# Queries and keys of the second attention branch: two units of a projection in the wide form

## The reference, cut to what matters

```
proj = einsum('bsd,dc->bsc', x, w_in)          # 1024 -> all columns of
(qa, ka, va, qi, ki, wi, qf, kf, vf, fg, qs, ks_, vs, gates) = split(proj)
o_a = dsa_attention(qa, ka, va, qi, ki, wi)    # first branch: 64 keys per query, picked by an index score
o_b = forgetting_attention(qf, kf, vf, log_f)  # second branch
o_c = stick_breaking_attention(qs, ks_, vs)    # third branch
```

## Time and profile before

| | |
|---|---|
| Median of 3 runs | 1476.67 us (1475.9 to 1478.39) |
| The profiled execution's own time | 1476.4 us |
| Its span | 1474.6 us |
| PE busy | 1462.3 us, 99% of the span |
| DVE busy | 1205.8 us, 82% |
| ACT busy | 884.6 us, 60% |
| POOL busy | 168.7 us, 11% |
| Instructions | 19013 |

### The profile page before, as it was taken

How to read it: one execution, slowest core, us unless ns; L and a number is a source line. 1 busy time by engine, 2 the same in 40 slices (tenths; PEclk the granted TensorE clock), 3 DMA queues, 4 the chain that set the end, 5 groups by cost and what they waited for, 6 DMA issues and landing times.

```text
span 1474.6 us, 19013 instructions
## 1 busy us (share of the span) xinstructions
PE 1462.3 (99%) x7628; PEld 1244.4 (84%) x7628; DVE 1205.8 (82%) x1246; ACT 884.6 (60%) x925; POOL 168.7 (11%) x177
## 2 busy tenths in 40 slices
PE   9999999999999999999999999999999999999997
PEld 8888888888888888888888888888998888899995
DVE  7899877789998899886566789986796466789998
ACT  6666666566666666554434666666555666367664
POOL 0000210200002000033030200002002200020001
PEclk9999999999999999999999999999999999999998
DMA  9898554589848688455445688955454434488761
GB/s 368 263 334 254 184 200 172 208 284 274 278 172 326 210 288 299 171 203 204 172 143 175 271 245 283 309 159 192 170 172 172 143 143 152 162 337 263 221 213 52
DMA packets 49768, 325.85 MB, mean 221 GB/s; under 512 B 5920, under 2 KB 6368, under 8 KB 12944
## 3 DMA queue, kind: packets, MB, share of 16 engines
q1 hardware_dynamic: 38592, 270.35, 47.8%
q0 software_dynamic: 9280, 50.53, 16.0%
q10 hardware_dynamic: 1808, 3.74, 0.7%
HBM read 282.60 MB, written 1.05 MB: 192 GB/s over the span
## 4 chain that ended last, share of the span: by engine, by line
PE 92%; DVE 4%; DMA 3%; issue 1%; ACT 0%; DVEq 0%; SPq 0%; ACTq 0%; POOLq 0%
PE psum L2367 14%; PE psum L2371 14%; PE psum L2370 14%; PE psum L2614 6%; PE psum L2617 6%; PE psum L2613 6%; PE psum L2503 5%; PE psum L2476 4%; PE psum L2510 3%; PE psum L2480 2%; PE psum L2399 2%; PE psum L2412 2%; PE psum L2405 2%; PE psum L3145 2%; PE psum L3142 2%; PE psum L3141 2%
## 5 line engine op out<-in xcount | busy, mean ns | idle before, releaser
L1399 DVE TENSOR_TENSOR weights_lo<-weights_raw,weights_hi 128x2048 fp32r<-128x2048 f32 (+1 forms) x166 | 369.2, 2225 | 136.3 <-ACT weights_hi L738 134.6
L738 ACT ACTIVATE weights_hi<-weights_raw 128x2048 fp32r<-128x2048 f32 (+1 forms) x179 | 319.4, 1787 | 164.8 <-PE psum L2371 101.5
L2367 PE MATMUL psum<-weights_hi,operand 128*128 128x512 f32 x384 | 151.5, 394 | 0.0
L2370 PE MATMUL psum<-weights_lo,operand 128*128 128x512 f32 x384 | 150.0, 391 | 0.0
L1399 DVE TENSOR_TENSOR weights_lo<-weights_raw_more,weights_hi 128x2048 fp32r<-128x2048 f32 (+1 forms) x74 | 145.3, 1967 | 4.6 <-ACT weights_hi L738 4.6
L2371 PE MATMUL psum<-weights_hi,operand 128*128 128x512 f32 x352 | 137.3, 390 | 0.0
L738 ACT ACTIVATE weights_hi<-weights_raw_more 128x2048 fp32r<-128x2048 f32 (+1 forms) x84 | 132.0, 1586 | 5.2 <-DVE weights_raw_more L2220 3.6
L2367 PE MATMUL psum<-weights_hi,hidden_hi 128*128 128x512 f32 x300 | 119.1, 397 | 0.9 <-DVE weights_lo L1399 0.9
L2370 PE MATMUL psum<-weights_lo,hidden_hi 128*128 128x512 f32 x300 | 117.3, 391 | 0.0
L2371 PE MATMUL psum<-weights_hi,hidden_lo 128*128 128x512 f32 x300 | 117.2, 391 | 0.0
L2367 PEld LDWEIGHTS psum<-weights_hi,operand 128*128 128x128 f32 x384 | 72.2, 188 | 15.7 <-issue 1.2
(11 more groups left out here) (486 smaller groups left out, 3456.6 us busy)
## 6 DMA issues: line engine op xcount, KB each, us to landing
weights_raw<-in_weights SPq DMA_DIRECT2D x154, 1024.0 KB, 4.8
weights_raw_more<-in_weights SPq DMA_DIRECT2D x76, 1024.0 KB, 9.1
normalised<-in_weights SPq DMA_DIRECT2D x16, 1024.0 KB, 4.9
weights_raw<-weights_raw POOLq DMA_DIRECT2D x12, 1024.0 KB, 11.9
ln_rows<-in_weights SPq DMA_DIRECT2D x8, 1024.0 KB, 10.3
weights_raw_more<-ln_rows POOLq DMA_DIRECT2D x8, 1024.0 KB, 7.1
ln_rows<-in_ln_rows POOLq DMA_DIRECT2D x16, 512.0 KB, 6.1
ln_rows<-normalised POOLq DMA_DIRECT2D x4, 1024.0 KB, 16.5
```

What stands on the lines that cost most here:

```text
L738: nc.scalar.activation(hi[:, rest], whole[:, rest], ACT.Copy).then_inc(hi_split, 1)
L1399: nc.vector.tensor_tensor(lo_of(n), raw_of(n), hi_of(n).bitcast(F32), ALU.subtract).then_inc(lo_split, 1)
L2367: mm(out, a_hi, b_hi, start=start, stop=False, skip_group_check=True)
L2370: mm(out, a_hi, b_lo, start=False, stop=False, skip_group_check=True)
```

## The change

Units 5 and 6 get the wide form. On PE `features_unit` is replaced by `features_halves`, with `first_logits` at the same place, three quarters into unit 6. On ACT one copy per unit is replaced by two half copies around the split of the next tile. On DVE four sums come into the list, at the places that the diff shows. The counts of the semaphores follow.

```diff
-        wide = ["gla2", "gla3", "ret1", "ret2", "ret3", "ret4", "sec1", "sec2", "sec8", "sec9"]
+        wide = ["gla2", "gla3", "ret1", "ret2", "ret3", "ret4", "sec1", "sec2", "sec5", "sec6", "sec8", "sec9"]
-        pair_count = lambda u: 12 if u == 0 else (13 if u < 8 else 14) + u // 2
+        pair_count = lambda u: 12 if u == 0 else (13 if u < 7 else 14 if u < 8 else 15) + u // 2
...
# ACT
-            part(5, as_pair(a_q[:, 1]), HEAD_DIM ** -0.5)
+            halves(5, (pairs[1], pairs[0]), a_q[:, 1], HEAD_DIM ** -0.5)
             split_hi(n + 14)
-            part(6, as_pair(a_k[:, 1]))
+            halves(6, (pairs[1], pairs[0]), a_k[:, 1])
             split_hi(n + 16)
...
# DVE
             split_lo(n + 12)
+            halves(5, 0, a_q[:, 1], HEAD_DIM ** -0.5)
             pick_largest(1, 4)
             split_lo(n + 13)
+            halves(5, 1, a_q[:, 1], HEAD_DIM ** -0.5)
             pick_largest(0, 4)
             split_lo(n + 14)
+            halves(6, 0, a_k[:, 1])
             pick_largest(0, 4)
...
             split_lo(n + 15)
+            halves(6, 1, a_k[:, 1])
             logits(0, 0)
...
# PE
-            unit(5, features_unit)
+            features_halves(n + 10, (pairs[1], pairs[0]), awaits(1, 14, 0, 15), "sec5")
...
-            unit(6, features_unit, between={6: first_logits})
+            features_halves(n + 12, (pairs[1], pairs[0]), awaits(1, 15, 0, 16), "sec6", between={6: first_logits})
             unit(7, tokens_unit, between={4: third_logits})
-            features_halves(n + 16, pairs, awaits(0, 16, 1, 16), "sec8")
+            features_halves(n + 16, pairs, awaits(0, 17, 1, 17), "sec8")
             turn_p(0, range(0, 4))
-            features_halves(n + 18, pairs, awaits(0, 17, 1, 17), "sec9", between={4: lambda: turn_p(0, range(4, 8))})
+            features_halves(n + 18, pairs, awaits(0, 18, 1, 18), "sec9", between={4: lambda: turn_p(0, range(4, 8))})
```

## The result

The changed kernel takes 1479.82 us in the median of 15 runs (1477.51 to 1481.5), the kernel before 1476.14 in 15 runs beside it (1475.9 to 1478.39): a ratio of 1.0023, 95% interval 1.0016 to 1.0029. It is slower, by 3.7 us. The forecast was 1478.1, with a term for PE saved and a larger one for PE waiting; the waiting is there, and dearer than worked out. The profiled execution took 1481.5 us, the longest of the fifteen, span 1479.7, granted clock 0.996 in the mean.

A forecast was written before the change was run, and what follows sets the result against it. The prediction took PE, busy 99% of the span, to bound the kernel. 0.66 us saved and 2.04 waited made +1.4 on the median 1476.67, so 1478.1 us, range 1475.2 to 1480.4 (its own 1476.9 to 1479.4).

The forecast's parts named there:

- a larger one for PE waiting: Before the transposes after unit 8: PE waits 2.04 us for POOL, 1.4 us later than before.
- The saving on PE: Units 5 and 6: wide matmuls save 0.34 us per unit, 0.68 for both; PE reaches the transposes 0.66 early.
- The rival in which the pairs save almost nothing: Units 5 and 6: saving only 0.2 us instead of 0.68, nothing waits, 1476.5 us; chance 0.03.
- ACT and SP: Units 5 and 6: two half copies of 0.60 us per unit are free on ACT; SP's tile loads still arrive in time.
- DVE's lateness: From unit 5 on: four added sums of 0.61 us leave DVE 0.97 us late at the low part of tile 16.
- First sum's wait: DVE in unit 5, behind the low part of tile 12: waits 0.47 us for ACT's half copy.
- the 1.86 us wait for tile 16: DVE's wait for ACT's high part of tile 16 goes, as ACT's copy comes 1 us earlier.
- POOL's seventh instruction: POOL after unit 8: only its last instruction, due at 1118.30, falls behind tile 19's subtraction (1118.02), ending at 1120.55; the one running finishes.
- An empty PE of 2 us need not cost clock: PE's wait before the transposes: granted clock stays, since 2 us without a matmul at the span's end still had 1.00.
- the rival in which POOL is caught twice: After unit 8: subtractions of tiles 19 and 20 both hold POOL, PE goes on 4.6 us later, 1481.3 us; chance 0.09.
- The sum: Whole kernel: 0.66 us saved on PE against 2.04 waited, +1.4 us on the median, giving 1478.1 us.
- the slower rival: After unit 8: POOL held at two DVE subtractions, PE 4.6 us later than before, 1481.3 us; chance 0.09.

The follow-up runs named there:

- the one profile with 1.84 us of empty PE: Kernel before the change, with nine scale-and-add instructions repeated on DVE ahead of the first softmax logits; 1478.23 us, ratio 1.0015.

## Why the prediction was right or wrong

- **The saving on PE: right.** Units of 11.17 and 13.29 us for the 11.18 and 13.28 that it took; PE ready for the transposes at 1118.86, less 0.27 is 1118.59, for 1118.61. The rival in which the pairs save almost nothing falls, and with it the estimate from the page TensorE: Matmul & The Clock Gate of the Trainium skill, whose section gives that gap for an isolated matmul.
- **ACT and SP: nothing there, right.** No wait in units 5 to 7 in the changed kernel's trace.
- **DVE's lateness: right to a tenth of a microsecond.** First sum's wait 0.38 (0.47 worked out), the 1.86 us wait for tile 16 gone, its low part at 1099.87 (1099.92), that of tile 18 at 1111.90 (1111.96), of tile 19 at 1118.00 (1118.02).
- **POOL: right in place, short by a quarter of a microsecond.** The step let POOL's seventh instruction finish since it would be running when DVE starts: "The one that runs is finished, the next ends 0.24 after DVE". It started 0.04 us ahead of DVE and was held all the same, so two were caught and POOL ended at 1120.83 on before's scale instead of 1120.55. PE's wait is 2.30 us and not 2.04. The earlier trace rows was the wrong case to go by: its first instruction, 0.12 us ahead of DVE, ran through in 0.37 us. Before's trace had the nearer case, in the first of POOL's last twelve, 0.02 us ahead of DVE's 1111.18 and held:

```profile
1111.16 2.58 POOL L681 TENSOR_SCALAR att_p<-att_p,att_sum 128x256 f32<-128x256 f32 x1 [2.33 <-DVE att_sum L2006]
```

- **The clock: wrong, and the larger miss.** The step that failed is "An empty PE of 2 us need not cost clock", by which a fall was put at nothing. In both profiles of the changed kernel the granted clock fell to 0.50 for 3.4 us behind the wait, which cost PE 1.61 us in the first; filling the wait kept it at 1.00. The earlier trace rows showed a clock of 1.00 while PE was empty and 0.50 in the stretch behind, and was read as leave for a wait of 2 us. A wait ends where that row went on: what PE runs first behind it is in the stretch at risk. The prediction names a fall of the clock only under the rival in which POOL is caught twice.
- **The sum.** +1.4 was put down: -0.7 + 2.0. Measured in the trace: -0.7 + 2.3 + 1.6 = +3.2, and +3.7 in the medians. POOL was caught at one subtraction only, so the slower rival did not come. The measured 1479.82 lies inside the stated range, 1475.2 to 1480.4, but above the forecast's own, 1476.9 to 1479.4, and above the 1479.6 from which the prediction would call a run slower, to which it gave 0.13. The microsecond added to the range took it in, and no term of the sum: that is luck. The place and the order of events were foreseen; the price was not.

## What to carry to other kernels

Work added to an engine that has time to spare is priced where its lateness meets a neighbour: follow it to the next long instruction that shuts another engine out, and compare start times there, since with margins of a few tenths of a microsecond both engines' shifts count (here POOL's came later by 0.9 us, DVE's earlier by 0.7). Price a wait of an otherwise full TensorE with what the clock may take behind it, here 1.6 us on top of 2.3 in the trace. When such a meeting is found, turning the order of two instructions may cost nothing: one wait on DVE took the whole loss away.

## What the runs showed of the hardware

- The clock fell to the 1.2 GHz level behind an empty PE of 2.1 us (from the end of one matmul to the start of the next) in both profiles of the changed kernel, for 3.4 us each time, once from the first transpose on and once from about a microsecond behind it; in the one profile with 1.84 us of empty PE it stayed at 1.00. PE was full ahead of all three.
- A POOL instruction that had started 0.04 us ahead of DVE's subtraction of one SBUF tile from another took 2.52 us instead of 0.35, as this row of POOL in the changed kernel shows:

```profile
1118.23 2.52 POOL L681 TENSOR_SCALAR att_p<-att_p,att_sum 128x128 f32<-128x128 f32 x1
```

That such a DVE instruction shuts POOL's reads out is what the Trainium skill says in SBUF — State Buffer, section Who interferes with whom, and the trace agrees. The section adds that the one that issues first holds the shared ports for its whole instruction; by the starts in this profile POOL was first and was held, so recorded starts 0.04 us apart do not tell who holds them.

- The traces show how far ahead POOL's recorded start had to be. In the second profile of the changed kernel it led by 0.08 us and was held:

```profile
1117.48 2.53 POOL L681 TENSOR_SCALAR att_p<-att_p,att_sum 128x128 f32<-128x128 f32 x1
...
1117.56 2.29 DVE L1399 TENSOR_TENSOR weights_lo<-weights_raw,weights_hi 128x2048 fp32r<-128x2048 f32 x1 [1.69 <-ACT weights_hi L738]
```

With the transposes later it led by 0.10 us and ran through, and DVE's subtraction took 2.42 us instead of 2.29:

```profile
1118.37 0.38 POOL L681 TENSOR_SCALAR att_p<-att_p,att_sum 128x128 f32<-128x128 f32 x1
...
1118.47 2.42 DVE L1399 TENSOR_TENSOR weights_lo<-weights_raw,weights_hi 128x2048 fp32r<-128x2048 f32 x1 [1.68 <-ACT weights_hi L738]
```

Against this subtraction, in the nine traces here, leads of 0.02, 0.04 and 0.08 us were held, and those from 0.10 us up ran through.
